# Gate and up products of a ConvFFN with the weights stationary and the tokens moving

## What is computed

```python
h = rmsnorm(x, norm_g[i, 2])
def conv_ffn(h, w_gate, w_up, conv_w, conv_b, w_down):
    g_pre = h @ w_gate
    gp = jnp.pad(g_pre, ((0, 0), (CONV_WIDTH - 1, 0), (0, 0)))   # causal, width 3, over tokens
    gc = conv_b
    for k in range(CONV_WIDTH):
        gc = gc + gp[:, k:k + S] * conv_w[k]
    return (jax.nn.silu(gc) * (h @ w_up)) @ w_down
```

## Time and profile before

| | us |
|---|---|
| median of three runs (2313.46 to 2314.83) | 2313.47 |
| the profiled execution, its own time | 2314.53 |
| its span, first to last instruction | 2312.7 |
| mean granted clock of TensorE | 0.995 |

### The profile page before, as it was taken

How to read it: one execution, slowest core, us unless ns; L and a number is a source line. 1 busy time by engine, 2 the same in 40 slices (tenths; PEclk the granted TensorE clock), 3 DMA queues, 4 the chain that set the end, 5 groups by cost and what they waited for, 6 DMA issues and landing times.

```text
span 2312.7 us, 26784 instructions
## 1 busy us (share of the span) xinstructions
PE 2281.9 (99%) x10618; PEld 1889.9 (82%) x10618; DVE 1300.7 (56%) x1664; ACT 1200.4 (52%) x1642; POOL 19.8 (1%) x21
## 2 busy tenths in 40 slices
PE   8999999999999999999999999999999999999998
PEld 7888888788888888888888877778888888888886
DVE  6555455655555555444566677656555555554444
ACT  6545664654555555443574544446455545544443
POOL 0000000000000000000030000000000000000000
PEclk9999999999999999999999999999999999999999
DMA  8555556566566656676655843355656656666664
GB/s 278 176 159 163 168 167 194 152 187 186 182 190 185 183 181 213 187 227 200 193 181 172 270 132 94 126 164 171 184 182 190 185 183 183 191 205 193 193 195 137
DMA packets 116205, 422.36 MB, mean 183 GB/s; under 512 B 13297, under 2 KB 13297, under 8 KB 115313
## 3 DMA queue, kind: packets, MB, share of 16 engines
q1 hardware_dynamic: 115472, 417.98, 58.7%
q10 hardware_dynamic: 432, 2.15, 0.2%
q0 software_dynamic: 176, 0.53, 0.1%
HBM read 418.51 MB, written 2.10 MB: 182 GB/s over the span
## 4 chain that ended last, share of the span: by engine, by line
PE 94%; DVE 4%; ACT 1%; DMA 0%; issue 0%; SPq 0%; DVEq 0%; ACTq 0%
PE bank L497 91%; PE bank L606 2%; DVE lo L1029 1%; PE bank L588 1%; DMA raw<-in_mem 0%; DVE ps L1236 0%; ACT hi L782 0%; DVE st L1092 0%; ACT ps L973 0%; DVE blkf L1197 0%; DVE ropeD L1089 0%; DVE x L1117 0%; DVE o L1136 0%; ACT ps L969 0%; ACT psc L969 0%
## 5 line engine op out<-in xcount | busy, mean ns | idle before, releaser
L1029 DVE TENSOR_TENSOR lo<-raw,hi 128x1024 fp32r<-128x1024 f32 x776 | 943.7, 1224 | 850.7 <-ACT hi L782 848.6
L497 PE MATMUL bank<-hi,h 128*128 128x512 f32 x3904 | 1242.0, 394 | 2.8 <-DVE h L1055 1.7
L782 ACT ACTIVATE hi<-raw 128x1024 fp32r<-128x1024 f32 x776 | 819.1, 1060 | 737.1 <-PE bank L497 716.7
L497 PEld LDWEIGHTS bank<-hi,h 128*128 128x128 f32 x3904 | 735.4, 188 | 154.9 <-issue 2.5
L497 PE MATMUL bank<-lo,h 128*128 128x512 f32 x1952 | 762.1, 390 | 0.0
L497 PE MATMUL bank<-hi,mid 128*128 128x512 f32 x1408 | 434.2, 389 | 0.0
L497 PEld LDWEIGHTS bank<-lo,h 128*128 128x128 f32 x1952 | 368.1, 189 | 72.5
L497 PEld LDWEIGHTS bank<-hi,mid 128*128 128x128 f32 x1408 | 264.4, 188 | 54.7
L497 PE MATMUL bank<-lo,mid 128*128 128x512 f32 x704 | 273.9, 389 | 0.0
L497 PE MATMUL bank<-hi,o 128*128 128x512 f32 x512 | 164.1, 394 | 1.1 <-DVE o L1137 1.1
L497 PEld LDWEIGHTS bank<-lo,mid 128*128 128x128 f32 x704 | 132.2, 188 | 27.4
(11 more groups left out here) (196 smaller groups left out, 1034.8 us busy)
## 6 DMA issues: line engine op xcount, KB each, us to landing
raw<-in_gate SPq DMA_DIRECT2D x176, 512.0 KB, 4.3
raw<-in_up SPq DMA_DIRECT2D x176, 512.0 KB, 3.6
raw<-in_down SPq DMA_DIRECT2D x176, 512.0 KB, 4.2
raw<-in_in SPq DMA_DIRECT2D x136, 512.0 KB, 3.9
raw<-in_out SPq DMA_DIRECT2D x64, 512.0 KB, 3.6
raw<-in_mem SPq DMA_DIRECT2D x31, 512.0 KB, 4.4
raw<-in_cmp SPq DMA_DIRECT2D x16, 512.0 KB, 4.2
x<-in_x ACTq DMA_DIRECT2D x2, 1024.0 KB, 8.8
```

The lines of the kernel that those rows point to most:

```text
L497: return mm(out, lhsT, rhs, start=first, stop=last, skip_group_check=True)
L782: act(hi[k][:, 0:w], raw[k][:, 0:w], ACT.Copy).then_inc(hi_done, 1)
L1029: tt(lo[k][:, 0:w], raw[k][:, 0:w], hi[k][:, 0:w].bitcast(F32), ALU.subtract).then_inc(lo_done, 1)
```

## The change

The gate and up chunks get a kind of their own, `ffn`, whose pieces are made by `features`. The stationary operand is now a 128x128 block of weights, the moving operand 256 tokens of `h`. A piece is 24 matmuls of 256 columns: two contraction tiles, four blocks of 128 output features, three terms into one place. The result has features on the partitions and tokens along the bank, two blocks in a bank, so the chunk is not transposed. `evac` and `turn` are gone from the FFN, and `convA`, `convB` and `gateup` read other places.

The norm's root is now needed as a row along the tokens. `rxrow` makes it once per FFN: PE transposes `rx`, broadcast over 128 columns, into bank 5, and DVE copies it to `rxb`, 128x256. DVE multiplies the gate chunk by it on the way from the bank to `st` (`gatescale`), and the SiLU's result by it in place (`rowscale`), so that `gateup` can take the up chunk from its bank as it is.

```diff
-            s.run(s.chunk(f"g{l}.{i}", f"gate{l}", i, "h", (0, 1), gate=("h", 1 + 2 * l) if i == 0 else None))
-            s.run(s.chunk(f"u{l}.{i}", f"up{l}", i, "h", (2, 3)))
+            s.run(s.chunk(f"g{l}.{i}", f"gate{l}", i, "h", (0, 1), kind="ffn", gate=("h", 1 + 2 * l) if i == 0 else None))
+            s.run(s.chunk(f"u{l}.{i}", f"up{l}", i, "h", (2, 3), kind="ffn"))
...
+            if k % 2 == 0:
+                do(last + feeds[7] + 3, "rxrow", k + 1, on="pe dve")
...
-            stage(f"g{l}.{i}", up + 1, "ffn", banks=(4, 5))
-            do(up + 1, "convA", n, on="act")
-            do(up + 2, "convB", n, on="dve")
-            do(up + 4, "silu", n, on="act")
-            stage(f"u{l}.{i}", after + 1, "ffn", banks=(6, 7))
-            do(after + 1, "gateup", n, on="dve")
...
+            g = at(f"g{l}.{i}") + (2 if i == 0 else 0)
+            do(g, "gatescale", n, on="dve")
+            do(g + 1, "convA", n, on="act")
+            do(g + 2, "convB", n, on="dve")
+            do(g + 3, "silu", n, on="act")
+            do(g + 4, "rowscale", n, on="dve")
+            do(at(f"u{l}.{i}"), "gateup", n, on="dve")
...
+                    if c.kind == "ffn":
+                        take(b, mf_done if c.name[0] == "u" else gs_done, 2 * (PAIRS * int(c.name[1]) + c.ci) + t + 1)
...
+            def features(c, p, n):
...
+                for q in range(2):
+                    kt = c.kts[p] + q
+                    for f in range(4):
+                        w_hi, w_lo = (w[k][:, q * W + f * P:q * W + (f + 1) * P] for w in (hi, lo))
+                        out = B[c.banks[f // 2]][:, f % 2 * T:(f % 2 + 1) * T]
+                        add(out, w_hi, h[:, kt, 0, :], p == 0 and q == 0 and f % 2 == 0, False)
+                        add(out, w_hi, h[:, kt, 1, :], False, False)
+                        m = add(out, w_lo, h[:, kt, 0, :], False, p == 7 and q == 1)
+                m.then_inc(piece_done, 1)
...
+            def rxrow(f):
+
+                take(5, rxb_done, f // 2 + 1)
+                pe_.wait_ge(rx_done, f + 1)
+                for t in range(2):
+                    m = tr(B[5][:, half(t)], rx[:, t:t + 1].broadcast_to((P, P)), ident)
+                m.then_inc(rxb_ready, 1)
...
+            def gatescale(n):
+                l, i = divmod(n, PAIRS)
+                dve.wait_ge(rxb_done, l + 1)
+                dve.wait_ge(piece_done, PLAN.at(f"g{l}.{i}") + 1)
+                for b in range(2):
+                    by_row(st[:, 0, b, :], B[b][:, :]).then_inc(gs_done, 1)
+
+            def rowscale(n):
+                for b in range(2):
+                    dve.wait_ge(silu_done, 2 * n + b + 1)
+                    by_row(cv[:, b, :], cv[:, b, :]).then_inc(row_done, 1)
```

More of the change, by code:

```diff
@@ L227, in ffn_steps @@
             n = PAIRS * l + i
-            after = at(f"g{l}.{i + 1}", 0) if i + 1 < PAIRS else at(f"d{l}0", 0)
-            up = at(f"u{l}.{i}", 0)
-            stage(f"g{l}.{i}", up + 1, "ffn", banks=(4, 5))
-            do(up + 1, "convA", n, on="act")
-            do(up + 2, "convB", n, on="dve")
-            do(up + 4, "silu", n, on="act")
-            stage(f"u{l}.{i}", after + 1, "ffn", banks=(6, 7))
-            do(after + 1, "gateup", n, on="dve")
-            do(after + 2, "midhi", n, on="act")
-            do(after + 3, "midlo", n, on="dve")
+            g = at(f"g{l}.{i}") + (2 if i == 0 else 0)
[5 more added lines that the diff above has]
+            do(at(f"u{l}.{i}"), "gateup", n, on="dve")
+            do(at(f"u{l}.{i}") + 1, "midhi", n, on="act")
+            do(at(f"u{l}.{i}") + 2, "midlo", n, on="dve")
         post(2 * l + 1, [f"d{l}{c}" for c in range(4)], range(5, 13) if l == 0 else None)
@@ L331, in build @@
         mxs, nb, sums, guard, rs, wgt = (sb(n, [P, 8]) for n in ("mxs", "nb", "sums", "guard", "rs", "wgt"))
+        rxb = sb("rxb", [P, T])
         pos, posf = sb("pos", [P, 2], I32), sb("posf", [P, 2])
@@ L377, in build @@
         x_sq, xtot_done, root_x, rx_done = sem("x_sq"), sem("xtot_done"), sem("root_x"), sem("rx_done")
+        rxb_ready, rxb_done, gs_done, row_done = sem("rxb_ready"), sem("rxb_done"), sem("gs_done"), sem("row_done")
         cv_done, conv_done, silu_done, mf_done = sem("cv_done"), sem("conv_done"), sem("silu_done"), sem("mf_done")
@@ L503, in take_banks @@
                 for t, b in enumerate(c.banks):
-                    if c.name in where_staged:
+                    if c.kind == "ffn":
+                        take(b, mf_done if c.name[0] == "u" else gs_done, 2 * (PAIRS * int(c.name[1]) + c.ci) + t + 1)
+                    elif c.name in where_staged:
                         take(b, staged, 2 * where_staged[c.name] + t + 1)
@@ L540, in wide @@
                         m = add(out, u[:, kt, 1, half(t)], w_hi, False, last)
+                m.then_inc(piece_done, 1)
+            def features(c, p, n):
+                if p == 0:
+                    take_banks(c)
+                if c.gate:
+                    pe_.wait_ge(h_done, 8 * c.gate[1] + p + 1)
+                k = n % RING
+                for q in range(2):
[6 more added lines that the diff above has]
+                        m = add(out, w_lo, h[:, kt, 0, :], False, p == 7 and q == 1)
                 m.then_inc(piece_done, 1)
@@ L597, in turn @@
                 for i, b in enumerate(banks):
[L598 to L602, removed]
+                    take(b, copied, 2 * COPIED.index(k) + i + 1)
                     for q in range(2):
@@ L736, in nsaC @@
                 m.then_inc(pv_ready, 1)
-            kinds = {"wide": wide, "gates": gates, "cmp": compress}
-            does = {"msum": msum, "turnx": turnx, "turn": turn, "memA": memA, "memB": memB, "memC": memC,
+            kinds = {"wide": wide, "ffn": features, "gates": gates, "cmp": compress}
+            does = {"msum": msum, "turnx": turnx, "rxrow": rxrow, "turn": turn, "memA": memA, "memB": memB, "memC": memC,
                     "stickA": stickA, "stickB": stickB, "stickC": stickC, "gatesT": gatesT, "hidT": hidT, "cmp": cmp,
@@ L911, in convA @@
                 for b in range(2):
-                    act_.wait_ge(turned, 2 * FFN[2 * n] + b + 1)
+                    act_.wait_ge(gs_done, 2 * n + b + 1)
                     for q in range(2):
                         f = 4 * i + 2 * b + q
-                        m = act(cv[:, b, q * T:(q + 1) * T], B[4 + b][:, q * T:(q + 1) * T], ACT.Identity,
+                        m = act(cv[:, b, q * T:(q + 1) * T], st[:, 0, b, q * T:(q + 1) * T], ACT.Identity,
                                 scale=conv[:, l, f, 2:3], bias=conv[:, l, f, 3:4])
@@ L1151, in stickC, with rxrow, by_row @@
                 split_out(hd, B[5][:, 0:T], ho_done)
+            def rxrow(f):
+                dve.wait_ge(rxb_ready, f // 2 + 1)
+                copy(rxb[:], B[5][:, 0:T]).then_inc(rxb_done, 1)
+            def by_row(out, a):
+                two = [z.rearrange("p (q t) -> p q t", q=2) for z in (out, a)]
+                return tt(two[0], two[1], rxb[:].rearrange("p (o t) -> p o t", o=1).broadcast_to((P, 2, T)), ALU.mult)
+            def gatescale(n):
[8 more added lines that the diff above has]
+                    by_row(cv[:, b, :], cv[:, b, :]).then_inc(row_done, 1)
             def convB(n):
@@ L1160, in convB @@
                             to = cv[:, b, at + d:at + T]
-                            m = stt(to, B[4 + b][:, at:at + T - d], conv[:, l, f, 2 - d:3 - d], to, ALU.mult, ALU.add)
+                            m = stt(to, st[:, 0, b, at:at + T - d], conv[:, l, f, 2 - d:3 - d], to, ALU.mult, ALU.add)
                         if d == 1:
@@ L1166, in gateup @@
             def gateup(n):
+                l, i = divmod(n, PAIRS)
+                dve.wait_ge(piece_done, PLAN.at(f"u{l}.{i}") + 1)
                 for b in range(2):
-                    dve.wait_ge(silu_done, 2 * n + b + 1)
-                    dve.wait_ge(turned, 2 * FFN[2 * n + 1] + b + 1)
-                    tt(mf[:, b, :], B[6 + b][:, :], cv[:, b, :], ALU.mult).then_inc(mf_done, 1)
+                    dve.wait_ge(row_done, 2 * n + b + 1)
+                    tt(mf[:, b, :], B[2 + b][:, :], cv[:, b, :], ALU.mult).then_inc(mf_done, 1)
             def midlo(n):
@@ L1248, in _ @@
                     "rope": rope, "ychunk": ychunk, "post": post, "xadd": xadd, "mem_square": mem_square, "memA": memA, "memC": memC, "stickA": stickA,
-                    "stickC": stickC, "convB": convB, "gateup": gateup, "midlo": midlo, "gatesT": gatesT,
+                    "stickC": stickC, "rxrow": rxrow, "gatescale": gatescale, "rowscale": rowscale, "convB": convB, "gateup": gateup, "midlo": midlo, "gatesT": gatesT,
                     "windows": windows, "hidT": hidT, "cmp": cmp, "nsaA": nsaA, "nsaS": nsaS, "nsaB": nsaB, "nsaC": nsaC}
```

## The result

| | before | after |
|---|---|---|
| median of four runs each, us | 2313.52 | 2330.16 |
| lowest to highest, us | 2313.46 to 2314.83 | 2330.14 to 2330.75 |
| span of the profiled execution, us | 2312.7 | 2328.4 |

The changed kernel is slower: the ratio is 1.0071, with a 95% interval of 1.0054 to 1.0089. The forecast was 2276 us with a range up to 2302, so the prediction was wrong in its sign. The time is near that of rival 2, 2333 us.

The account below looks back on a forecast made before the run. PE was taken to bound the kernel, busy 99% of the span. From 2314.5 us: -39.2 for transposes, 0 for matmuls, +0.5 for the norm's row, +1.2 for first pieces, 2277.0; median forecast 2276 us, range 2270 to 2302.

Parts of the forecast that it names:

- rival 2: Gate and up matmuls: the 0.0134 us excess is paid per matmul, 0.1201 us each, +57 us, 2333 us; chance 0.11.
- Matmuls: the same columns in twice as many: FFN pieces: 24 matmuls of 256 columns at 0.1133 us cost the same 2.720 us as 12 of 512; term 0.
- The bound above, 0.1163: Upper end for one 256-column matmul, from the compression product's bursts of eight: +25 us in the FFNs.
- The weight loads: FFN matmuls: full loads every 0.111 us stay hidden under the 0.1133 us stream, by 2 ns.
- decision point of 0.1178: Price in us of a 256-column matmul from which 38 us over 8448 matmuls eat the gain of the removed transposes.
- first mechanism: FFN matmuls: the 0.0134 us over the bare columns is paid per matmul whatever its length.
- other wording: FFN matmuls: load and matmul hamper one another to the same amount, 0.0134 us each.
- Rival 1: FFN stream never settles, small disturbances keep 256-column matmuls at 0.1163 us: 2301 us, or 2307 at 0.117; chance 0.18.
- The extra 1.2 us for the first pieces: Start of each FFN, while h is fed: transposes of x disturb seven pieces of 256-column matmuls; +1.2 us.
- Rival 3: Gate and up matmuls: fixed price of 0.0025 us for each of 4224 more, +10.6 us, 2287 us; chance 0.04.
- The turns: FFN chunk transposes on PE: 44 removed at 0.89 us each, -39.2 us.
- rival 4: Late lo in the FFN: DVE and ACT chain 3 us longer, PE waits, 22 us, 2298 us; chance 0.03.

Follow-up runs that it names:

- e2: Changed kernel with only the gate and up matmuls put back to 12 of 512 columns, no transposes: 2275.64 us, ratio 0.9831 against the kernel before.
- e3: Kernel before with only the gate and up matmuls changed to 24 of 256 columns, weights stationary, transposes kept: 2368.53 us, ratio 1.0235.
- The grids: Three kernels of bare matmul bursts, computing nothing of the reference, varying loaded and moving columns; fp32r with 256 moving: 113.3 ns at 32 loaded, 120.0 at 128.
- e1: Kernel of fifteen bursts of 96 matmuls alone on the chip, nothing of the reference; fp32r, 256 moving columns, full load: 0.120 us each.

## Why the prediction was wrong

**The step that failed** is "Matmuls: the same columns in twice as many", with its "the term is 0". The runs showed +56 us in its place, by the 120.0 ns of the trace; e2 and e3 gave 54.5 and 54.2. I took 0.1133 us from the earlier trace rows, where 36 columns are loaded, and carried it to matmuls that load 128. The grids show that this is the cheap corner: at 256 moving columns 32, 64, 80 and 112 loaded columns cost 113.3 ns (96: 116.0, 16: 116.7), a full load 120.0. The row itself was read at its best place, too. All 48 of these matmuls, from here to the last at 1233.15, take (1233.15 - 1227.71) / 47 = 0.1157 us each, and only the end of the stream goes at 0.1133:

```profile
1227.71 0.40 PE L497 MATMUL bank<-h,hi 128*36 128x256 f32 x2
```

"Half of 0.2267 is 0.1133" looked like a second witness and was an accident of two numbers with different excess: 13.4 over 213.3 with a full load, 6.7 over 106.7 with a small one. The bound above, 0.1163, came from a row with 60 loaded columns and was no bound either. No row of the trace before had fp32r matmuls of 256 columns with full loads, much as the text of rival 2 says; its end of the range should have stood open for that reason, and its chance should have been far above 0.11. Why a matmul with a full load costs 120.0 ns is not known; e2 and e3 show that this price is the loss.

**The weight loads** were treated as a separate limit: either they are under the stream's pace and hidden, or they are not. Their pace was right (0.111 us, again 0.111 in e1), and it gave no safety: at 256 moving columns the matmuls with a full load go at 0.120, slower than either pace. Whether the load itself does it, or the 128 partitions written, is not shown; bf16 matmuls write as many and go at 0.109.

**Rival 2** gave 0.1201 us a matmul and 2333 us; 0.1200 and 2330.2 were measured. Its decision point of 0.1178 was passed. Its first mechanism, the price per matmul whatever its length, holds for full loads at 256, 320, 384 and 512 columns to 0.1 ns, roughly at 240, 248 and 288 (11.7 to 12.0) and 448 (16.0), and not for smaller loads. Its other wording, load and matmul hampering one another, fits that the load matters at 256 columns; at 320 and 384 it doesn't matter. Neither tells the reason. That the total came out so near to 2333 is in part luck: the amount, 0.0134 us, was taken from 512 columns and is the one that 256 happen to have.

**Rival 1** falls: it had disturbances of a 0.1133 stream, and here is an even one of 0.1200 with 3164 equal distances, alone on the chip too. The extra 1.2 us for the first pieces wasn't there: they take 2.88 us like all others.

**Rival 3.** bf16 matmuls of 256 columns go at 109.2 ns and those of 512 at 215.8 within their burst, an excess of 2.5 ns, where fp32r has 13.3 with full loads. Plain fp32 shows 192 matmuls of 256 columns at (191.98 - 150.54) / 192 = 0.2158 us each; that would be 2.5 ns over two cycles a column, but no run here shows what such a matmul is made of. The Trainium skill (TensorE: Matmul & The Clock Gate, Back-to-back issue gap) gives 2.5 ns over N / 2.4 GHz, and that for a matmul taken by itself. The bf16 bursts agree though they are streams; fp32r doesn't at any of the lengths measured. This rival's 2.5 ns for each matmul more were 6.7 here, so its 2287 us falls too.

**What was right.** The turns: 39.2 us forecast, 38.7 in e2. `rxrow`: 0.22 us in the chain against 0.25. No wait for DVE, ACT, banks or transfers in the FFN, hence rival 4 falls; the clock at 1.00; PEld near 100%. DVE is at 59% where 66% was forecast: the pair of chunks is longer (46.1 us instead of 43.5), and the busy times that I added up overlap a little where instructions of DVE follow one another. That had no effect on the time. The pieces that I had ending at 441.8 and 444.5 are the eighth and ninth, not the ninth and tenth: the tenth, behind which `rxrow` stands, ended at 447.18 before and at 445.66 after, so there was more time for `rx` than I wrote.

## What to carry to other kernels

In fp32r count the matmuls as well as the columns, and take the price of one from a row with the same type, the same moving length and the same number of loaded columns; a row that differs in one of the three was no bound here. In this kernel turning the operand around paid only where the moving side stayed long: join what multiplies the same stationary block (hi and lo side by side), keep matmuls of one length and type together, and give the small correction term to bf16. That loads alone can go faster than the matmuls (0.111 against 0.1133 us) does not show that the two together keep the faster matmul pace.

## What was not expected of the hardware

The pace of fp32r matmuls doesn't rise smoothly: with full loads 112.0, 115.0, 120.0 and 131.7 ns at 240, 248, 256 and 288 columns, and at 256 columns 116.7, 113.3, 113.3, 120.0, 116.7, 120.0, 120.0 with 16, 32, 112, 116, 120, 124, 128 loaded. 512 columns are slower with a small load (231.7 ns at 32) than with a full one (226.7). After a change of length from 256 to 512 the next five fp32r matmuls are 1 to 9 ns slower, after bf16 most of the next nine. Alternating the lengths one by one cost 353 ns a pair where both wrote one bank and 346.6 where each had its own. The cause of none of these was found, and the full kernel was not tried with other sizes of load.
